# GpSimd rounds eleven weight units of the odd layer in quarters of 512 columns

## What is computed

```python
q, k, v, qi, ki, wi, gate_b, gate_c, hd = split_cols(h @ w_in, ODD_SPLITS)   # 1024 x 2628
score = einsum('bqhk,bqh->bqk', relu(qi . ki), wi)      # indexer, 4 heads
_, idx = top_k(score, 256)                              # keys that each query attends to
att = softmax attention of q over the selected k, v     # 8 heads
out = concatenate([att, gate_b * conv(gate_c * hd)]) @ w_out
```

## Time and profile before

| | |
|---|---|
| median of three runs | 3036.26 us (3028.46 to 3036.68) |
| span of the profiled execution, first to last instruction | 3034.6 us |
| TensorE (PE) busy | 2819.9 us, 93% |
| VectorE (DVE) busy | 1368.5 us, 45% |
| GpSimd (POOL) busy | 1036.0 us, 34% |
| ScalarE (ACT) busy | 745.4 us, 25% |
| chain that ended last | PE 73%, DVE 17%, ACT 5%, issue 4% |
| L1702, 93 times | 339.1 us, mean 3647 ns |
| L1705, 93 times | 468.3 us, mean 5035 ns |

### The profile page before, as it was taken

How to read it: one execution, slowest core, us unless ns; L and a number is a source line. 1 busy time by engine, 2 the same in 40 slices (tenths; PEclk the granted TensorE clock), 3 DMA queues, 4 the chain that set the end, 5 groups by cost and what they waited for, 6 DMA issues and landing times.

```text
span 3034.6 us, 38739 instructions
## 1 busy us (share of the span) xinstructions
PE 2819.9 (93%) x16281; PEld 2558.3 (84%) x16281; DVE 1368.5 (45%) x1908; ACT 745.4 (25%) x1227; POOL 1036.0 (34%) x359
## 2 busy tenths in 40 slices
PE   5999999989999999999978677789999999999998
PEld 4998744479899999999966677667899999999998
DVE  5113488735433323323348999533453323333234
ACT  3111477721110010100125562245311100100101
POOL 4332344404333334333332223480133334333431
PEclk7999999979999999999989888899999999999999
DMA  5110300011111111111111100210111111111111
GB/s 173 42 42 29 113 1 1 1 58 42 42 42 55 41 41 41 55 41 41 53 61 34 36 28 28 35 26 1 59 55 42 42 41 41 46 51 41 41 42 58
DMA packets 96239, 134.02 MB, mean 44 GB/s; under 512 B 17393, under 2 KB 81969, under 8 KB 95634
## 3 DMA queue, kind: packets, MB, share of 16 engines
q1 hardware_dynamic: 95570, 115.41, 12.1%
q10 hardware_dynamic: 576, 17.30, 1.4%
HBM read 113.16 MB, written 18.73 MB: 43 GB/s over the span
## 4 chain that ended last, share of the span: by engine, by line
PE 73%; DVE 17%; ACT 5%; issue 4%; SPq 1%; DMA 0%; POOL 0%; another core or an unknown queue 0%; DVEq 0%; ACTq 0%; POOLq 0%
PE PS L261 58%; DVE reach L1354 2%; DVE reach L1355 2%; PE PS L1222 2%; PE PS L1184 2%; PE PS L854 1%; PE PS L823 1%; DVE xT L349 1%; DVE hnf L474 1%; DVE rbuf L338 1%; ACT rbuf L318 1%; ACT hid L320 1%; PE PS L1198 1%; DVE pair L872 1%; PE PS L1125 1%
## 5 line engine op out<-in xcount | busy, mean ns | idle before, releaser
L261 PE MATMUL PS<-h,w_sp 128*128 128x352 f32 (+1 forms) x5256 | 893.5, 330 | 111.4 <-ACT Z L1270 52.9
L261 PEld LDWEIGHTS PS<-h,w_sp 128*128 128x128 f32 (+1 forms) x5256 | 873.2, 193 | 124.0 <-ACT Z L1270 54.7
L1702 POOL TENSOR_TENSOR w_sp<-stage,ones 128x2048 fp32r<-128x2048 f32 x93 | 339.1, 3647 | 1670.2 <-PE PS L261 1613.2
L261 PE MATMUL PS<-hid,w_sp 128*128 128x352 f32 x4608 | 756.4, 324 | 7.4 <-DVE xT L349 7.4
L261 PEld LDWEIGHTS PS<-hid,w_sp 128*128 128x128 f32 x4608 | 743.4, 188 | 16.1 <-DVE xT L349 16.1
L261 PE MATMUL PS<-hz,w_sp 128*128 128x352 f32 x3456 | 567.7, 323 | 0.0
L261 PEld LDWEIGHTS PS<-hz,w_sp 128*128 128x128 f32 x3456 | 558.7, 188 | 0.0
L1705 POOL TENSOR_TENSOR w_sp<-stage,w_sp 128x2048 fp32r<-128x2048 f32 x93 | 468.3, 5035 | 7.3
L349 DVE TENSOR_TENSOR xT<-PS,xT 128x1056 f32<-128x1056 f32 x256 | 319.0, 1256 | 336.2 <-PE PS L261 336.2
L318 ACT ACTIVATE rbuf<-rbuf 128x1056 f32<-128x1056 f32 x64 | 69.7, 1089 | 1247.6 <-DVE rbuf L338 1247.6
L338 DVE SCALAR_TENSOR_TENSOR rbuf<-PS,rstd 128x1056 f32<-128x1056 f32 x64 | 80.5, 1258 | 505.6 <-PE PS L261 505.5
(11 more groups left out here) (262 smaller groups left out, 2289.0 us busy)
## 6 DMA issues: line engine op xcount, KB each, us to landing
stage<-in_w_ffn SPq DMA_DIRECT2D x64, 1024.0 KB, 5.1
stage<-in_w_in_even SPq DMA_DIRECT2D x10, 1024.0 KB, 5.0
stage<-in_w_in_odd SPq DMA_DIRECT2D x10, 1024.0 KB, 5.0
x_spill<-xT ACTq DMA_DIRECT2D x2, 4224.0 KB, 11.9
xT<-x_spill ACTq DMA_DIRECT2D x2, 4224.0 KB, 12.7
xtok<-in_x_prompt SPq DMA_DIRECT2D x8, 512.0 KB, 7.4
stage<-in_w_out_even SPq DMA_DIRECT2D x4, 1024.0 KB, 9.1
stage<-in_w_out_odd SPq DMA_DIRECT2D x4, 1024.0 KB, 13.4
```

The costliest lines, as they stand in the source:

```text
L261: mm = pe.matmul(out[0:m, c, :], lhs, rhs(k, b)[:, c * CH:(c + 1) * CH], start=(k == 0 and n == 0), stop=(k == nk - 1 and n == 2))
L1702: pool.tensor_tensor(w_sp[:, s, 0, :], stage[:, s, :], ones[:, 0:1].to_broadcast([P, UN]), ALU.mult).then_inc(w_hi_done, 1)
```

## The change

Units 48 to 58 (`U_OIN + 2` to `U_OOUT + 1`) are split by a new function. It makes the high part in four instructions of 512 columns and the low part in four. The four of a half follow each other without a wait, and only the last of each half counts its semaphore. All other units keep `split`.

```diff
+            def split_pieces(u):
+
+                s, q = u % 2, UN // 4
+                pool.wait_ge(w_stage[s], 16 * (u // 2 + 1))
+                pool.wait_ge(job_done, last_job(u - 2) + 1)
+                for i in range(4):
+                    c = slice(i * q, (i + 1) * q)
+                    hi = pool.tensor_tensor(w_sp[:, s, 0, c], stage[:, s, c], ones[:, 0:1].to_broadcast([P, q]), ALU.mult)
+                hi.then_inc(w_hi_done, 1)
+                pool.wait_ge(w_hi_done, u + 1)
+                for i in range(4):
+                    c = slice(i * q, (i + 1) * q)
+                    lo = pool.tensor_tensor(w_sp[:, s, 1, c], stage[:, s, c], w_sp[:, s, 0, c].bitcast(F32), ALU.subtract)
+                lo.then_inc(w_split, 1)
+
...
             split(U_OIN)
             pool_norm(pool, 2)
-            for u in range(U_OIN + 1, U_OOUT + 2):
-                split(u)
+            split(U_OIN + 1)
+            for u in range(U_OIN + 2, U_OOUT + 2):
+                split_pieces(u)
             pool_odd(pool)
```

## The result

The changed kernel takes 3014.41 us (median of 4 runs, 3011.26 to 3018.09), against 3035.78 for the kernel before it (4 runs, 3028.46 to 3036.68): 0.9942 of it, 95% interval 0.993 to 0.9954. That is 21.4 us less. The forecast was 3017 us, in a range of 3009 to 3031.

What follows compares the result with a forecast made beforehand. VectorE, held up by GpSimd's instructions, was taken to bound units 48 to 57, except TensorE's scoring products. Gains 7.0 + 2.2 + 7 + 3.1 = 19.3 us off 3034.6 gave 3015.3; median 1.7 higher: 3017 us, range 3009 to 3031.

Steps and rivals of the forecast that it cites:

- Part 1: GpSimd's pieces: 1.03 us each (high), 1.28 (low); 1.0 us more per unit, lock held 7.4 us instead of 7.8.
- the opening: Start of each GpSimd instruction, before it takes the lock: VectorE was given 0.22 us to slip in an operation.
- Part 2: Bit search, units 51 to 55: VectorE's stall falls from 6.4 to 5.0 us each, gain 7.0, between 0 and 9.
- Part 3: Bit search, unit 50: stall falls from 7.7 to 5.5 us, gain 2.2, between 1.7 and 2.7.
- its walk: Unit 50's pieces followed in turn against VectorE's operations, starting 1.1 us into a bit: 5.5 us of stall together.
- Part 4: Scoring stage, units 48 and 49: VectorE gets more steps done and TensorE runs ahead, gain 7 us, between 3 and 9.
- Step 16: VectorE's sixteenth step of the scoring stage: done at about 1614.7 us instead of 1619.4, 4.7 us earlier.
- Part 5: Mask stage, units 56 and 57: stalls of 6.9 and 7.4 us become 5.2 and 6.0, gain 3.1, between 2 and 4.
- What costs nothing: Later w_split and longer GpSimd units, unit 58 included, stay covered by slack; without cover, attention starts up to 1 us late.
- A: Rival, chance 0.1: GpSimd keeps the lock through a half's four pieces, so the kernel is slower, 3041 to 3045 us.
- B: Rival, chance 0.17: every small VectorE operation of a bit meets its own piece; gain 8 us in all, 3028 us.
- C: Rival, chance 0.03: GpSimd waits for VectorE at each piece, TensorE then waits for w_split; 3040 us and more.

Runs made afterwards that it cites:

- the first experiment: Only units 48 and 49 split in quarters, against the kernel before the change: 3022.71 us against 3030.42, 0.9971.

## Why the prediction was right or wrong

**What bounds the stretch.** Right: with the stalls gone, a microsecond of VectorE was a microsecond of the bit search (175.4, the measured length less the measured stalls).

**Part 1 (the pieces themselves).** Right in the durations: 1.04 and 1.29 us where nothing was in the way, for 1.03 and 1.28. Wrong in the opening. The sum went by 0.22 us, taken from three rows of 0.26, 0.21 and 0.15. The pieces that follow without a wait start every 1.00 us at 1.04 each and let no second small operation by: L1377 and L1378, 0.2 us apart, each met a piece of their own. L1377 began 0.10 us behind the recorded start of its piece and still stood until that piece's end.

**Part 2 (units 51 to 55).** This is the step that failed in size. It said 4.9 us of stall and took 5.0; the restarts give 5.7 rising to 6.7, so that the gain was 1.7 us rather than 7.0, near the end "no gain" of its own bounds (0 to 9). Its own sign of being wrong, that the spacing of the restarts stays as it is, came true for units 54 and 55. Three assumptions were wrong. Pieces 1 and 2 were to cost 0.15 us beside L1355; L1372 and L1376 took 0.8 there at unit 55. L1354's first block didn't slip into the opening between the halves (1.86 us for 0.75, though it is recorded 0.02 us ahead of the piece). And the place at which a unit starts in a bit isn't fixed, as the step said, but moves from 2.7 to 3.7 us. Longer openings didn't repair it, so their length isn't the term that matters; the eighths point to how much of its own work VectorE gets done beside a unit.

**Part 3 (unit 50).** Right in the number, partly by luck: TensorE's restart behind it came 44.3 us after the start of unit 48's products, against 46.8, 2.5 us for a forecast of 2.2 (the terms of its walk add up to 5.4, not 5.5). The walk starts 1.1 us into a bit, but with the scoring stage changed too the unit started 2.6 us into it and cost 5.2 us. With units 50 to 55 changed alone it started where the step said and cost 5.8, a gain of 1.9.

**Part 4 (scoring).** Right in kind and a little low: 8.4 us for 7. Step 16 gained 5.3 us (4.7 forecast), and what came back behind it, with TensorE ahead, 3.0 (2.3 forecast). TensorE's granted clock in the window rose from 0.69 to 0.89, not quite to the 1 that it expected. This part is more than half of the change's effect, and stood alone in the first experiment.

**Part 5 (masks).** Right: 2.6 for 3.1, and 3.4 with the part alone, both within 2 to 4. Where no unit is split beside it the stage takes 40.5 us, so its stalls were 14.2 us before and 11.7 after, for 14.3 and 11.2 in the step.

**What costs nothing.** Right: the projections took 49.0 us in both. GpSimd was still done with unit 57 before the masks were.

**Sum.** 15.1 us by the stages against 19.3, so the forecast of 3017 was met by a difference of 21.4 that has some 6 us too much in it. That the median came within 3 us of the forecast is luck to this extent: the faster stretch ahead of the change made up for what the bit search didn't give. In the experiments the kernel before had medians of 3029.6 to 3034.5, lower than the 3035.78 here; from those the changed kernel's 3014.41 would be 15 to 20 us away. The stages are the better measure, and by them the forecast was 4 us too hopeful.

**Rivals.** A (no opening between pieces) fell: pieces without a wait between them took turns with VectorE, and one of them took 1.75 us for 1.29. The Trainium skill, GPSIMD Engine Reference, section Instruction dispatch, says that completion doesn't hold back the next Pool instruction; the trace agrees (pieces of 1.04 us start 1.00 apart), but it gave VectorE its turn all the same. B (the pieces deal the same stall out) was nearly right for units 51 to 55, where 1.7 us came, and its 8 us in all are too few against 15.1. C (late weights) never came near.

## What to carry to other kernels

Where two engines share a lock that is held for an instruction, the price is read from the long rows of the *other* engine's smallest operations (4.03 us for seven columns), and busy shares don't show it. Cutting the long instructions deals out the turns more finely, and what that wins depends on what gets the turns. In the scoring stage each turn went to a step of about a microsecond (5.3 us of the 8.4), and TensorE, which had idled behind the stall, ran ahead (3.0). In the bit search half of the turns went to operations of seven columns and the others to blocks of 0.55 to 0.75 us, and units 54 and 55 gained nothing. That this is the reason for the difference is read from the rows and wasn't tried by itself. Before cutting, ask whether the held-up engine could do the work itself, or whether the work can be moved to where that engine waits anyway. Here that took 53 us off the three stages instead of 15, some 6 of them by the written-out loop.

## What the runs showed that was not expected

- Eighths beat quarters by 17.4 us by the totals (one run, on another chip), and by 2.8, 8.0 and 6.6 us in the three stages, though GpSimd's own time for a unit grows again.
- VectorE operations with an accumulated count (L1355) ran beside GpSimd's instructions at their usual 0.6 to 0.76 us in every kernel, while a plain compare of the same tile (L1354) was held up. L1354 is also the faster one: 0.53 ns a column (0.75 us for 1024, 0.55 for 640), where L1355 has 0.94 (0.73 us for 512, 0.61 for 384). The Trainium skill, SBUF — State Buffer, section SBUF: two separate sides, has VectorE's faster two-port forms and those with two SBUF inputs contend with GpSimd; the trace agrees, 1.86 us for 0.75.
- VectorE idles 0.39 us at the end of each pass of its loop, and ahead of L1376, where the loop waits against a register, 0.12 us instead of 0.03. Over the 32 bits the written-out form was 6.4 us shorter.
- The even layer's stretch ahead of the change differs by almost 14 us between profiles (1576.0 to 1589.6), with TensorE's granted clock between 0.66 and 0.83 in the same 60 us.
